# Mixture of experts: three instead of two last slots kept out of the adds to memory

## The reference

```
ids = g_idx * EXPERTS_PER_GROUP + e_idx
gates = jnp.sum(jax.nn.one_hot(ids, N_EXPERTS) * w_e[..., None], axis=-2)
y = jnp.zeros_like(h)
for e in range(N_EXPERTS):
    hid = jax.nn.silu(h @ wg[e]) * (h @ wu[e])
    y = y + gates[..., e:e + 1] * (hid @ wd[e])
...
x = x + mod_lat[:, 5] * hier_moe(modulate(rms_norm(x, norm_ffn_g[l]), mod_lat[:, 3], mod_lat[:, 4]), *moe_p)
return rms_norm(x, final_norm_g)
```

## Time and profile before

| | |
|---|---|
| median of 3 runs | 982.9 us (982.03 to 983.45) |
| profiled execution: time, span | 984.42 us, 982.5 us |
| PE busy | 860.6 us (88%) |
| DVE busy | 649.1 us (66%) |
| ACT busy | 421.8 us (43%) |
| POOL busy | 198.6 us (20%) |
| DMA | 196.72 MB, mean 200 GB/s |

### The profile page before, as it was taken

How to read it: one execution, slowest core, us unless ns; L and a number is a source line. 1 busy time by engine, 2 the same in 40 slices (tenths; PEclk the granted TensorE clock), 3 DMA queues, 4 the chain that set the end, 5 groups by cost and what they waited for, 6 DMA issues and landing times.

```text
span 982.5 us, 11517 instructions
## 1 busy us (share of the span) xinstructions
PE 860.6 (88%) x3617; PEld 603.1 (61%) x3618; DVE 649.1 (66%) x702; ACT 421.8 (43%) x516; POOL 198.6 (20%) x192
## 2 busy tenths in 40 slices
PE   5679999994979898999927899999999999999980
PEld 2255444441434455888826688788887888778860
DVE  2133569899698354443467879676886579955866
ACT  2243343531545252122234357445655357724543
POOL 1000290791000000000002123231141224432120
PEclk9889999996999999999967899999999999999995
DMA  8922510600522442255154879986996879975876
GB/s 288 359 50 107 178 58 26 210 0 22 192 65 85 171 172 86 107 193 198 81 192 151 299 229 376 314 250 177 374 377 183 282 257 384 359 244 148 273 237 255
DMA packets 91911, 196.72 MB, mean 200 GB/s; under 512 B 10739, under 2 KB 31345, under 8 KB 91884
## 3 DMA queue, kind: packets, MB, share of 16 engines
q1 hardware_dynamic: 83500, 165.99, 46.8%
q0 software_dynamic: 7056, 25.15, 10.3%
q10 hardware_dynamic: 1328, 5.24, 1.4%
HBM read 172.26 MB, written 24.64 MB: 200 GB/s over the span
## 4 chain that ended last, share of the span: by engine, by line
PE 55%; DVE 18%; DMA 12%; issue 7%; ACT 4%; DVEq 1%; POOL 1%; SPq 1%; POOLq 1%; ACTq 0%
PE bank L745 11%; PE bank L967 5%; PE bank L969 5%; PE bank L968 5%; DMA mixed_rows<-ysc,idg 4%; DMA mring<-in_mod_w 3%; PE bank L872 3%; PE bank L874 3%; PE bank L873 3%; PE bank L988 2%; PE bank L990 2%; PE bank L989 2%; DMA xg<-normed_rows,idg 2%; PE bank L789 2%; DVE gu L1547 2%
## 5 line engine op out<-in xcount | busy, mean ns | idle before, releaser
L745 PE MATMUL bank<-hT,wring 128*128 128x512 f32 x384 | 169.7, 601 | 2.6 <-ACT hT L1052 1.9
L1547 DVE TENSOR_TENSOR gu<-raw_gu,gu 128x2048 fp32r<-128x2048 f32 x64 | 145.5, 2287 | 32.2 <-ACT gu L1223 30.0
L967 PE MATMUL bank<-gu,xp 128*128 128x512 f32 x368 | 147.9, 402 | 3.5 <-issue 1.8
L1223 ACT ACTIVATE gu<-raw_gu 128x2048 fp32r<-128x2048 f32 x64 | 122.3, 1918 | 56.7 <-PE bank L969 48.3
L969 PE MATMUL bank<-gu,xp 128*128 128x512 f32 x368 | 145.1, 394 | 0.0
L968 PE MATMUL bank<-gu,xp 128*128 128x512 f32 x368 | 144.9, 394 | 0.0
L745 PEld LDWEIGHTS bank<-hT,wring 128*128 128x128 f32 x384 | 73.8, 193 | 93.7 <-issue 90.2
L1699 DVE TENSOR_TENSOR dn<-raw_dn,dn 128x1024 fp32r<-128x1024 f32 x64 | 75.9, 1221 | 10.7 <-ACT dn L1249 8.5
L967 PEld LDWEIGHTS bank<-gu,xp 128*128 128x128 f32 x368 | 70.2, 191 | 18.7 <-issue 2.2
L969 PEld LDWEIGHTS bank<-gu,xp 128*128 128x128 f32 x368 | 70.1, 190 | 15.3
L968 PEld LDWEIGHTS bank<-gu,xp 128*128 128x128 f32 x368 | 70.4, 191 | 14.1
(11 more groups left out here) (293 smaller groups left out, 1354.8 us busy)
## 6 DMA issues: line engine op xcount, KB each, us to landing
raw_gu<-in_expert_w_gate SPq DMA_DIRECT2D x64, 512.0 KB, 6.3
raw_gu<-in_expert_w_up SPq DMA_DIRECT2D x64, 512.0 KB, 7.9
raw_dn<-in_expert_w_down SPq DMA_DIRECT2D x64, 512.0 KB, 9.6
mring<-in_mod_w SPq DMA_DIRECT2D x20, 1024.0 KB, 5.4
wring<-in_w_in SPq DMA_DIRECT2D x12, 512.0 KB, 6.6
mslot<-in_mod_w SPq DMA_DIRECT2D x4, 1024.0 KB, 16.2
xt<-in_x ACTq DMA_DIRECT2D x2, 2048.0 KB, 11.5
dring<-in_dft SPq DMA_DIRECT2D x8, 512.0 KB, 4.0
```

The lines of the kernel that those rows point to most:

```text
L745: mm = pe.matmul(o_, wring[:, n % 3, k, :], src, start=k == 0, stop=k == KD - 1)
L967: pe.matmul(bank[g][:], x_hi, w_hi, start=k == 0, stop=False)
L1223: A_(gu[j][0][:], raw_gu[j][:], ACT.Copy).then_inc(s_hgu, 1)
L1547: tt(gu[j][1][:], raw_gu[j][:], gu[j][0][:].bitcast(F32), ALU.subtract).then_inc(s_logu[j], 1)
```

## The change

Three last slots instead of two are left out of the adds: the loop on POOL ends one slot sooner, so `s_end` comes after the add of slot W - 4, and SP may load `fx` then. The gather of slot W, which stood in POOL's last pass, now stands behind the memset that signals `s_end`. POOL needs W - 3 in a register (`W3`); it is computed in the tables (`inc3`) and loaded. A third tile `xl2` is gathered, summed, normed and written. On DVE all four `final_pair` stand first, then slots W - 3 and W - 2 are summed and normed together, then slot W - 1 is scaled, summed and normed. `fj`, where ACT writes the squares, shrinks to one old buffer to make room.

```
-                    with pool.If(2 * it + par + 2 < W):
+                    with pool.If(2 * it + par + 3 < W):
                         q = 2 * it + par
                         pool.wait_ge(s_xgt, 2 * q + 6)
                         gather(q + 3, 2 * q + 2)
...
             pool.memset(stat[:, 63:64], 0.0).then_inc(s_end, 1)
+            W3 = pool.value_load(tab[0:1, 3, 1:2], min_val=NE - 3, max_val=MAXT - 3)
+            pool.wait_ge(s_xgt, 2 * W3 + 6)
+            gather(W, 2 * W3 + 2)
+            for n in range(3):
+                link(pool.tensor_copy(idl[:, 0, n:n + 1], gid[:, bass.ds(W3 + n, 1)]))
+                link(pool.tensor_copy(idl[:, 1, n:n + 1], sid[:, bass.ds(W3 + n, 1)]))
             pool.wait_ge(s_gud, 4 * W)
-            for n in range(2):
-                pool.tensor_copy(idl[:, 0, n:n + 1], gid[:, bass.ds(W - 2 + n, 1)])
-                link(pool.tensor_copy(idl[:, 1, n:n + 1], sid[:, bass.ds(W - 2 + n, 1)]))
-            for n in range(2):
+            for n in range(3):
                 pool.indirect_dma_start(out=xl[n][:], out_offset=None, in_=x1_d[0:SEQ],
...
             pool.wait_ge(s_out, 16 * NT)
-            for n in range(2):
+            for n in range(3):
                 pool.wait_ge(s_fo, NT + n + 1)
...
-            final_pair(0)
-            final_pair(1)
+            for b in range(NT // 2):
+                final_pair(b)
             dve.wait_ge(s_ye, 2 * W)
-            last_sum(0, ysc[:, bass.ds(W % 2, 1)].rearrange("p a n -> p (a n)"))
-            final_pair(2)
+            for n in range(2):
+                last_sum(n, ysc[:, bass.ds((W + 1 + n) % 2, 1)].rearrange("p a n -> p (a n)"))
+            final_mean(4)
+            for n in range(2):
+                final_row(NT + n, xl[n][:]).then_inc(s_fo, 1)
             dve.wait_ge(s_xgt, 2 * W + 2)
             scale_y(W - 1, ylast[:])
             dve.wait_ge(s_ye, 2 * W + 2)
-            last_sum(1, ylast[:])
-            final_pair(3)
-            for n in range(2):
-                final_mean(4 + n)
-                final_row(NT + n, xl[n][:]).then_inc(s_fo, 1)
+            last_sum(2, ylast[:])
+            final_mean(5)
+            final_row(NT + 2, xl[2][:]).then_inc(s_fo, 1)
```

On ACT the root of the first two `xl` tiles is taken once, after both are squared (`final_root(4)`), and that of the third by itself. In the tables POOL gets three small instructions more, ahead of the gather of slot 1:

```
+            inc3 = row(1480, NE)
+            link(pool.memset(inc3, -3.0))
+            link(pool.tensor_tensor(inc3, inc3, inc1, ALU.add))
...
+            pool.tensor_copy(tab[0:1, 3, 1:2], inc3[:, NE - 1:NE]).then_inc(s_tab, 1)
```

More of the change, by code:

```diff
@@ L242, in build @@
         tab = at("tab", [1, 4, TAB], I32, o); o += 640
-        idl = at("idl", [P, 2, 2], I32, o); o += 32
+        idl = at("idl", [P, 2, 3], I32, o); o += 32
         hp = at("hp", [P, 2, KE, P], F32R, o)
@@ L273, in build @@
         fx = [at(f"fx{t}", [P, D], F32, (Y0, H0)[t // 2 % 2] + 8192 * (t // 4) + 4096 * (t % 2)) for t in range(NT)]
-        fj = [at(f"fj{n}", [P, D], F32, GU[n][0]) for n in range(2)]
-        xl = [at(f"xl{n}", [P, D], F32, GU[2 + n][0]) for n in range(2)]
+        fj = [at(f"fj{n}", [P, D], F32, GU[0][0] + 4096 * n) for n in range(2)]
+        xl = [at(f"xl{n}", [P, D], F32, GU[1 + n][0]) for n in range(3)]
         s_prow = sem("constants_and_parameters_in")
@@ L423, in build @@
         MCH = D // 256
-        FCOLS = [(28, 29), (30, 31), (32, 33), (34, 35), (36,), (37,)]
+        FCOLS = [(28, 29), (30, 31), (32, 33), (34, 35), (36, 37), (38,)]
         EORD = [EPG * g + j for j in range(EPG) for g in range(NG)]
@@ L581, in _ @@
             sp.wait_ge(s_out, 16 * NT)
-            sp.wait_ge(s_xl, 64)
+            sp.wait_ge(s_xl, 96)
         @block.gpsimd
@@ L681, in _ @@
             link(pool.tensor_copy(tab[0:1, 2, :], lT))
-            pool.tensor_copy(tab[0:1, 3, 0:1], inc1[:, NE - 1:NE]).then_inc(s_tab, 1)
+            link(pool.tensor_copy(tab[0:1, 3, 0:1], inc1[:, NE - 1:NE]))
+            pool.tensor_copy(tab[0:1, 3, 1:2], inc3[:, NE - 1:NE]).then_inc(s_tab, 1)
             pool.wait_ge(s_gid, 2)
@@ L1324, in _ @@
                     final_root(t // 2)
-            for n in range(2):
+            for n in range(3):
                 act.wait_ge(s_xla, n + 1)
                 final_square(NT + n, xl[n][:])
-                final_root(4 + n)
+                if n:
+                    final_root(3 + n)
         @block.vector
@@ L1780, in last_sum @@
             def last_sum(n, y):
-                dve.wait_ge(s_xl, 32)
+                dve.wait_ge(s_xl, 48)
                 tt(xl[n][:], xl[n][:], y, ALU.add).then_inc(s_xla, 1)
```

## The result

| | before | after |
|---|---|---|
| median of 20 runs | 983.56 us (980.26 to 987.29) | 986.47 us (983.79 to 990.17) |
| ratio to before, 95% interval | | 1.0027 (1.0017 to 1.0038) |
| span of the profiled execution | 982.5 us | 983.0 us |

The account below looks back on a forecast made before the run. The chain named the `fx` loads (11.95 us), with ACT and DVE in the loop almost until their arrival. Loads -0.3, DVE's stage +3.7, last write -1.0 give +2.4; gather +1.7; 982.9 + 4.1 = 987.0 us, range 984.3 to 990.3.

Parts of the forecast that it names:

- DVE's stage: DVE's final rows at the kernel's end: 23.8 us instead of 20.1, longer by 3.7.
- the case I held most likely: PE waits 0.7 to 2.7 us for the moved gather's rows near the loop's end; chance 0.52.
- in time: Rival: the moved gather lands before PE needs it, leaving only the longer tail, +2.4 us, 985.3; chance 0.20.
- The loads, sooner by 12 us, worth 0.3: `fx` loads start at 934.6 instead of 946.6, but ACT's loop end limits the gain to 0.3 us, bounds 0 to 0.45.
- POOL's last write, 1.0 us back: POOL's last write of rows starts 0.3 us after DVE's end instead of 1.29, bounds 0 and 1.29.
- The moved gather, +1.7: Slot 23's gather on POOL starts at 934.7, lands at 942.3; PE waits 1.7 us, bounds 0 and 3.4.
- the 0.7 us that I worked out beside it: PE's wait for the moved gather if DVE held POOL's copy for one instruction only: 0.7 us instead of 1.7.
- The tables: Three small POOL instructions ahead of slot 1's gather: costed at nothing, 1 us if uncovered.
- Not slower: Rival: the final stage starts once its data is there, first rows before 953; no change, 982.9 us; chance 0.12.

Follow-up runs that it names:

- e4: The changed kernel with ACT's and DVE's slot loops cut from 32 to 24 slots, for this data only: ratio to the kernel before 1.0003.
- e5: The kernel before with ACT's and DVE's slot loops cut from 32 to 24 slots, for this data only: ratio to the uncut kernel before 0.9989.
- e2: The changed kernel with DVE's three sums moved ahead of the third and fourth pair of final tiles: DVE's stage 21.17 us, ratio to before 1.0024.
- e1: The changed kernel with the gather of slot W put back ahead of the empty slots on POOL: ratio to the kernel before 1.0032.
- after_again: The changed kernel itself, unaltered, profiled and timed a second time beside its variants: ratio to the kernel before 1.0038.
- e6: The changed kernel with the memset that releases the `fx` loads held until the moved gather has landed: ratio to the kernel before 1.0023.
- e7: The changed kernel with the gather back, sums ahead of the last two pairs, and PE's, ACT's, DVE's and POOL's loops cut to 24 slots: ratio to before 0.998.
- e8: The kernel before with PE's, ACT's, DVE's and POOL's slot loops split into 24 and 8 slots, valid for all data: ratio to the unsplit kernel 0.998.
- e9: The changed kernel with the gather back, sums ahead of the last two pairs, and four engines' loops split into 24 and 8 slots: ratio to before 0.9984.

## Why the prediction was right, and which sizes were off

The direction and the main term, DVE's stage, were right; the forecast was +4.1 us, the runs give some +2.7 and the tails +3.0 and +3.5. Two things in it were luck or wrong. The 987.0 us forecast is only 0.5 from the 986.47 measured partly because the median of three runs that it was added to, 982.9, is 0.7 below that of 20 runs, 983.56. And the case I held most likely, PE late by 0.7 to 2.7 us for the moved gather, did not come: it was late by 0.0 to 0.5, which is the rival "in time" that I had given 0.20.

- **The loads, sooner by 12 us, worth 0.3.** By the tanh they start 12.0 us sooner. They were worth nothing: "to rows" is 4.85 in both kernels. The reasoning from the loop's own branch records held, and e4 against e5 shows it by experiment.
- **DVE's stage, 23.8 us.** Measured 23.75, with the two idle times of 1.21 at the means, as laid out. e2, which covers them, takes 2.6 us off.
- **POOL's last write, 1.0 us back.** It was 0.5: the write starts 0.80 behind DVE's end, not 0.3. I had taken the idle time between two DMAs that follow each other for the time from a semaphore to a DMA. This is a mis-sized term, by 0.5.
- **The moved gather, +1.7.** This is the step that failed in size. It was 0.5 us in one execution and 0.0 in the other, and e1 puts it at nothing. The step said "the copy ends at about 934.3 and the gather starts at 934.7", because at 844.38 a copy had been held over three subtractions. In after the copy was ready at 927.10, and it was held for 0.71 only, to the end of the subtraction then running (four of them take 4.62 us from 926.56, the first to about 927.8); the next instruction was held to the end of the second, and the DMA's own issue took 1.83. So the gather started by the tanh 2.6 us sooner than I had it, 0.9 us of it because the copy was ready sooner. Its landing of 8.8 was longer than my 7.6 and gave back 1.2 of that, which leaves the 0.4 to 0.5 of this execution. This is how the rule of the Trainium skill, SBUF — State Buffer, section "SBUF: two separate sides", would have it (a lock held for one instruction, not for a row of them), with the 0.7 us that I worked out beside it closer to the 0.0 and 0.5 measured. That closeness is in part luck too, since it has the gather start only a microsecond sooner and land in 7.6. Why the copy at 844.38 was held over three subtractions of the larger tiles while this one slipped in between subtractions of the smaller ones, no run here shows.
- **The tables.** The three small instructions take 0.10, 0.21 and 0.17 us in after, and the copy behind them ended at the same subtraction's end as before (2.25 us instead of 2.28). In after_again the last of the three took 2.34 us instead and the copy 0.17. From the memset that begins the tables to the gather of slot 1 it is 5.66 us before, and 5.71 and 5.80 us in these two, so they cost 0.1 us at most.
- **The rivals.** "In time" with its +2.4 is what after_again and e1 show, at +3.0. "Not slower" failed as said: it would have needed the final stage to begin with its data, and e4, where the loop's end is cut, is the kernel in which it does; there the ratio is 1.0003.

What makes the moved gather's landing 8.1 to 8.8 us (a size that I had put at 7.6 from a median) is for the most part in the trace of the kernel before, where I had not looked for it. Of the 21 gathers of the earlier trace rows, 19 were issued by POOL in about 1.0 us. Five of these, with a DMA busy share of 0.34 to 0.41 from issue to landing, took 4.3 to 4.5 us, and 13, with 0.94 to 1.06 by the profile's count, took 6.5 to 8.1; one with 0.75 took 4.5. The issue of two others was itself held, 2.05 and 2.06 us, and they took 5.5 with a share of 0.32. These are stretches from issue to landing of one gather of each kind in before, and of the moved one in after; the numbers in front are the stretch in us, its length, and the busy time of PE, PE's weight loads, DVE, ACT and POOL in us with the number of their instructions; the last three are PE's granted clock, the DMA engines' busy share and GB/s:

```profile
889.49:893.90 4.41, 4.41 (x22) 3.61 (x21) 0.48 (x1) 0.00 (x0) 1.01 (x1) 1.00 0.37 119
876.03:881.50 5.47, 5.47 (x27) 4.57 (x26) 4.18 (x5) 1.54 (x2) 3.13 (x4) 1.00 0.32 96
843.38:850.88 7.50, 5.46 (x25) 4.18 (x23) 7.50 (x5) 4.32 (x3) 7.50 (x2) 1.00 1.04 407
```

```profile
929.11:937.95 8.84, 8.60 (x38) 6.77 (x37) 4.57 (x7) 0.60 (x1) 3.03 (x7) 1.00 0.92 316
```

The moved gather meets both: a share of 0.92 and an issue of 1.83 us. As an estimate from these rows, busy DMA engines make about 3 us of its landing and the held issue about 1. With the `fx` loads held back in e6 the share is still 0.86 and the landing 8.1, where the only other transfers are the loads of the down weights; these started 1.3 us ahead of the gather in all five executions that have it moved. In its old place it was issued 4.0 to 4.7 us ahead of them and landed in 4.4 to 4.5 (before, e5, e7, e8, e9). No run took one of the two causes away by itself.

## What to carry to other kernels

A wait that the chain names may hide a second one that ends at the same moment: before paying for an earlier transfer, ask where the engines that need it are by then, and count the branches of empty loop passes too. When a reordering puts a sum right ahead of its own mean, price the other engine's part between them, here 1.2 us each time, since what used to stand there was cover. And when a useless transfer is moved later, look for who waits for it; here it was nearly free, by luck of a few tenths of a microsecond. A median over gathers mixes those beside loads with those beside none: for a landing time, take the gathers issued under the same traffic.

## What the runs showed that I had not expected

- Stepping over empty slots costs ACT 2.65 us for 8 slots (idle 2.80 against 0.15), 0.33 us a slot, on the path of every version whose early loads are in time and whose loops are whole. No other single edit of the study took as much off a tail (2.7 us, e4 against after_again).
- The last indirect DMA, for whose row of DVE the idle POOL waits, starts 0.80 us behind that row's end (0.79 to 0.80 in five executions), against 0.30 between two such DMAs in a row.
- A POOL copy can get in between two back-to-back subtractions of 128x1024 on DVE (held 0.56 to 0.94 us in five executions), though a copy had been held over three subtractions of 128x2048 for 6.68 us.
